# The last FFN's up-projection: seven products of quarters per block on halves of 256 tokens, in place of eight on 512 tokens

## The chip, the cores and the metric

The kernel runs on one core of one Trainium2 chip, as one launch. The metric is the device time in microseconds (us), and lower is better. Inputs and outputs are float32.

## What is computed

The reference is a two-layer backbone over 512 latent tokens and 256 context tokens, with a model width of 1024. Each layer holds an FFN, a mixing stage (DeltaNet heads and RWKV-7 heads) and a second FFN. In the second layer the context tokens leave the computation after the mixing stage, so the last of the four FFNs works on the 512 latent tokens alone:

```
def swiglu(h, w13, w2):
    gate, up = jnp.split(h @ w13, 2, axis=-1)
    return (jax.nn.silu(gate) * up) @ w2

h_lat = h_lat + 0.5 * m_lat[8] * swiglu(modulate(rms_norm(h_lat, norm_g[i, 2]), m_lat[6], m_lat[7]),
                                        ffn_w13[i, 1], ffn_w2[i, 1])
```

`w13` is 1024 x 5632 (gate and up, 2816 columns each) and `w2` is 2816 x 1024.

## The kernel before

**Layout.** Activations lie with model features on the 128 partitions and tokens along the free axis. A product of a 128x128 weight tile with up to 512 tokens is one matmul. To keep float32 accuracy every operand is split into a high part and a low part (both fp32r), and each product is made in three passes, high by high, high by low and low by high (`PASSES`). The high part is written by ScalarE (ACT, `act_piece`, L814) and the low part by VectorE (DVE, `dve_piece`, L821), which subtracts the high part from the raw weights in place.

**Blocks and parts.** The 2816 hidden features are 22 blocks of 128. The blocks are grouped into parts (`FF_PARTS`): part 0 has blocks 0 and 1, parts 1 to 5 have four blocks each. For each part TensorE (PE) first makes the blocks (the up-projection), then the part's share of the down-projection (`out`, L942), in two groups of four output tiles. DVE adds each output tile to `h` (`add`, L1201).

**Two ways of making a block.** The FFNs are numbered n = 0 to 3.
- The whole way (`whole_block`, L885 and L889): gate and up, eight weight tiles each, in three passes. In FFN 3, the one for which `lone(n)` is true, a product spans all 512 tokens: 2 x 8 x 3 = 48 matmuls of 512 columns for each block. In the other FFNs blocks 0 and 1 are made in this way, over two halves of 384 tokens.
- Seven pieces (`block`, L929): a block is a 2 x 2 matrix product (gate/up by lower/upper half of the model width) times (lower/upper width by left/right half of the tokens), and seven products of sums of quarters replace eight. Each piece is 4 tiles x 3 passes = 12 matmuls over half of the tokens, so a block is 84 matmuls. It is used for blocks 2 to 21 of FFNs 0, 1 and 2 (384 columns each).

**What the seven pieces need.** GpSimd (POOL, `pool_combine_weights`, L791 to L798) makes three weight combinations that PE uses and one step on the way, in four operations; ACT waits for the fourth before it splits the first piece. ACT and DVE split seven pieces for each block instead of four. At the head of an FFN DVE makes four sums of the activations (`sum_x`), and ACT and DVE split them (`x_high`, `x_low`); the last low part is made between the output additions of part 0. DVE needs nine combining operations over half of the tokens for each block (`combine`, L1116; `sum_2`, `sum_3`, ... `right_product`), where the whole way in FFN 3 needs one product over 512 tokens.

**Buffers and order.** Raw weights have two buffers, and a block's four loads of 256 KB (`block(f)` in `sp_ffn`, L733, issued by SyncE, SP) wait until PE has finished the block two before (`free`). The blocks in the first two places of a part are loaded partly under the down-projection of the part before (`early`, `late`); block 3 waits for the end of part 0's down-projection. Each engine has one fixed instruction order. For one block of seven pieces ACT's is

```
            def window(f):
                first_out(f)
                following(f, range(4))
                gate_left(f)
                following(f, (4, 5))
                gate_right(f)
                hidden_high(f, 9)
                following(f, (6,))
```

`following(f, ...)` splits the pieces of the next block. `first_out(f)` (L1005) copies the first product out of PSUM bank 0, and PE's fifth piece of the block, which writes that bank again, waits for it (`act_ready`). The sixth and seventh pieces wait for `sum_3` and `sum_4_and_up_right` on DVE. DVE's order is sums 2, 3, 4 and up-right, two splits, gate-left, two splits, up-left and left product, two splits, gate-right, right product, hidden-low, the last split.

Of the kernel before, what the change touches and what calls it, by code (L numbers as in the profile page):

```python
# [11 lines left out]
D_MODEL, SEQ, CTX, DEPTH, GRID_W = 1024, 512, 256, 2, 64  # L12
# [23 lines left out]
def build(nc, x, c, ctx, c_ctx, ada_w, ada_b, norm_g, ffn_w13, ffn_w2, w_in, dn_conv, dn_a_log, dn_dt_bias,  # L36
# [3 lines left out]
    with es:  # L40
# [578 lines left out]
        K_ORDER = tuple(k + KH * g for k in range(KH) for g in range(2))  # L619

        def lone(n):
            return n == 2 * DEPTH - 1

        def whole(n, f):

            return lone(n) or f < WHOLES
# [7 lines left out]
        def count_ffn():  # L634

            number, silus, sums, last_use = 0, 0, 0, {}
            for n in range(2 * DEPTH):
                sums += 0 if lone(n) else SUMMED_X
                load = 0
                for part, (f0, tiles) in enumerate(FF_PARTS):  # L640
                    for what in [*range(f0, f0 + tiles), (part, 0), (part, 1)]:
                        block = type(what) is int
                        piece_of[n, what], load_of[what] = number, load
                        load_first.append(number)
                        if block:
                            part_of[what] = part
                            silus_of[n, what], combined_of[n, what] = silus, sums
                            silus += 2 if lone(n) else 3 if whole(n, what) else 4
                            sums += 1 if lone(n) else 2 if whole(n, what) else 9
                        for j in range(pieces(n, what) if block else GROUP):  # L650
                            high = high_place(n, what, j)
                            high_free.append(last_use.get(high, -1) + 1)
                            last_use[high] = number
                            number += 1
                        load += 1
# [2770 lines left out]
```

## Time and profile before

| | |
|---|---|
| median of 3 runs | 3991.49 us (3987.45 to 3994.32) |
| profiled execution, span on the chip | 3987.0 us |
| PE busy | 3781.7 us (95%) |
| DVE busy | 2206.0 us (55%) |
| ACT busy | 1453.5 us (36%) |
| POOL busy | 760.9 us (19%) |
| mean granted TensorE clock | 0.991 |

The page gives the profiled execution's span alone, 4.5 us below the median of the runs. "Busy" is the share of the span in which an engine had an instruction in it. Matmuls are pipelined, so a matmul's own duration (389 ns for 512 columns) is longer than the distance from one start to the next. Times of rows are counted from the span's start. The granted clock is 1.00 at 2.4 GHz and 0.50 at 1.2 GHz. FFN 2 lies between about 2113 and 2667 us, FFN 3 between about 3595 and 3967 us.

### The profile page before, as it was taken

To read this page: it belongs to the slowest core of one execution; us is meant where nothing else is said; L and a number is where in the kernel's file an instruction comes from. 1 tells how busy PE (TensorE), PEld (TensorE's weight loads), DVE (VectorE), ACT (ScalarE), POOL (GpSimd) and SP (SyncE) were. 2 spreads that over 40 slices of the span, in tenths; PEclk is the share of its full clock that TensorE was granted. 3 is DMA by queue.
4 is the path that set the end of the run, shared out by engine and by line. 5 is a ranking of instruction groups with operands and counts; after the bars stand their busy time and mean duration, and the time that the engine had idled before them with its cause. 6 is when DMAs were issued, how large, how long until landed. Compare 5 with 4: busy or idle time off the path is not lost. (4 is left out here: it accounts for less than half of the span.)

```text
span 3987.0 us, 92656 instructions
## 1 busy us (share of the span) xinstructions
PE 3781.7 (95%) x40011; PEld 3300.6 (83%) x40011; DVE 2206.0 (55%) x3770; ACT 1453.5 (36%) x2512; POOL 760.9 (19%) x879
## 2 busy tenths in 40 slices
PE   7999999999988889999999999999999989889999
PEld 5899997877867768999998999987877857767887
DVE  4655556466465445755556555566465464454334
ACT  3333334344353333433234333343343253333223
POOL 1222210043024310222211222210242043300000
PEclk8999999999999999999999999999999999999999
DMA  6433332100200011332223333332100200023232
GB/s 209 129 108 113 107 96 87 37 18 2 77 11 4 5 72 43 118 98 89 85 67 116 106 109 113 106 106 59 28 2 18 71 2 5 33 84 89 81 114 66
DMA packets 409034, 287.17 MB, mean 72 GB/s; under 512 B 13438, under 2 KB 366180, under 8 KB 408164
## 3 DMA queue, kind: packets, MB, share of 16 engines
q1 hardware_dynamic: 408676, 281.86, 23.1%
q8 instruction: 290, 4.75, 0.5%
q14 instruction: 68, 0.56, 0.0%
HBM read 270.27 MB, written 11.53 MB: 71 GB/s over the span
## 5 line engine op out<-in xcount | busy, mean ns | idle before, releaser
L814 ACT ACTIVATE w_hi<-w_raw 128x512 fp32r<-128x512 f32 (+1 forms) x724 | 405.2, 612 | 649.6 <-POOL w_raw L798 349.2
L821 DVE TENSOR_TENSOR w_lo<-w_raw,w_hi 128x512 fp32r<-128x512 f32 (+1 forms) x724 | 484.9, 710 | 173.5 <-ACT w_hi L814 173.5
L929 PE MATMUL PS<-x_hi,w_hi 128*128 128x384 f32 x1680 | 562.7, 335 | 1.6 <-DVE hid_flat L1116 1.6
L929 PE MATMUL PS<-x_lo,w_hi 128*128 128x384 f32 x1680 | 561.3, 334 | 0.0
L929 PE MATMUL PS<-x_hi,w_lo 128*128 128x384 f32 x1680 | 561.2, 334 | 0.0
L1201 DVE SCALAR_TENSOR_TENSOR arena<-PS,mod,arena 128x256 f32<-128x256 f32 (+1 forms) x336 | 198.4, 632 | 332.5 <-PE PS L942 332.2
L1116 DVE TENSOR_TENSOR hid_flat<-hid_flat,PS 128x384 f32<-128x384 f32 (+1 forms) x454 | 246.2, 557 | 236.5 <-PE PS L929 153.3
L942 PE MATMUL PS<-hidden_hi,w_hi 128*128 128x256 f32 (+1 forms) x1232 | 342.3, 348 | 7.7 <-DVE hidden_lo L1168 5.7
L942 PE MATMUL PS<-hidden_hi,w_lo 128*128 128x256 f32 (+1 forms) x1232 | 337.5, 344 | 0.0
L942 PE MATMUL PS<-hidden_lo,w_hi 128*128 128x256 f32 (+1 forms) x1232 | 336.8, 343 | 0.0
L791 POOL TENSOR_TENSOR w_raw<-w_raw 128x512 f32<-128x512 f32 x60 | 85.0, 1417 | 1257.7 <-DMA w_raw<-in_ffn_w_dram 1172.9
L929 PEld LDWEIGHTS PS<-x_hi,w_hi 128*128 128x128 f32 x1680 | 315.4, 188 | 2.9 <-DVE hid_flat L1116 2.9
L929 PEld LDWEIGHTS PS<-x_lo,w_hi 128*128 128x128 f32 x1680 | 315.4, 188 | 0.2
L929 PEld LDWEIGHTS PS<-x_hi,w_lo 128*128 128x128 f32 x1680 | 315.4, 188 | 0.0
L942 PEld LDWEIGHTS PS<-hidden_hi,w_hi 128*128 128x128 f32 x1232 | 228.2, 188 | 64.5 <-issue 30.6
L942 PEld LDWEIGHTS PS<-hidden_lo,w_hi 128*128 128x128 f32 x1232 | 231.6, 188 | 29.1
L942 PEld LDWEIGHTS PS<-hidden_hi,w_lo 128*128 128x128 f32 x1232 | 231.4, 188 | 29.2
L2534 POOL TENSOR_TENSOR arena<-arena 128x256 f32<-128x256 f32 (+1 forms) x240 | 169.8, 728 | 262.5 <-ACT arena L2527 262.5
L1775 PEld LDWEIGHTS PS<-arena 128*128 128x128 f32 x1344 | 155.6, 192 | 16.9 <-DVE arena L2005 10.1
L1775 PE MATMUL PS<-arena 128*128 128x128 f32 x1344 | 161.4, 277 | 7.7 <-DVE arena L2005 7.7
L1302 PE MATMUL PS<-p_hi,pw_hi 128*128 128x256 f32 (+1 forms) x544 | 142.8, 344 | 4.6 <-DVE pw_lo L1295 2.9
L1302 PE MATMUL PS<-p_hi,pw_lo 128*128 128x256 f32 (+1 forms) x544 | 138.8, 337 | 0.0
(358 smaller groups left out, 7331.1 us busy)
## 6 DMA issues: line engine op xcount, KB each, us to landing
w_raw<-in_ffn_w_dram SPq DMA_DIRECT2D x512, 256.0 KB, 4.0
arena<-in_ada_w_dram SPq DMA_DIRECT2D x120, 512.0 KB, 5.9
arena<-in_w_in_dram SPq DMA_DIRECT2D x64, 512.0 KB, 3.9
arena<-in_ada_w_dram SPq DMA_DIRECT2D x6, 2048.0 KB, 14.0
arena<-in_w_out_dram SPq DMA_DIRECT2D x16, 512.0 KB, 4.3
h_save<-arena SPq DMA_DIRECT2D x16, 384.0 KB, 2.3
arena<-h_save SPq DMA_DIRECT2D x2, 3072.0 KB, 15.7
w_raw<-in_ffn_w_dram SPq DMA_DIRECT2D x32, 128.0 KB, 2.3
```

The costliest lines, as they stand in the source:

```text
L791: v.tensor_tensor(w[:, BOTH, :], w[:, DIFF, :], w[:, UP1, :], ALU.add).then_inc(weights_summed, 1)
L814: nc.scalar.activation(w_hi[:, high_place(n, what, j), 0:size], w_raw[:, load_of[what] % 2, place, 0:size], ACT.Copy).then_inc(w_high_read ...
L821: nc.vector.tensor_tensor(w_lo[:, b, place, 0:size], w_raw[:, b, place, 0:size], w_hi[:, high_place(n, what, j), 0:size].bitcast(F32), ALU ...
L929: mm = pe.matmul(PS[:, 4 * b + bank, 0:half], w[wo], x_split[xo][:, j, k, 0:half], start=(k == 0 and q == 0), stop=(k == KH - 1 and q == 2))
L942: mm = pe.matmul(PS[:, 2 * (k % 2) + s, 0:wd], w[wo], hid_split[xo][:, f, a0:a0 + wd], start=(f == 0 and q == 0), stop=(f == tiles - 1 and ...
L1116: v.tensor_tensor(out, x, y, op).then_inc(combined, 1)
L1201: ins = v.scalar_tensor_tensor(h[:, k, a0:a0 + w], PS[:, 2 * (k % 2) + s, 0:w], mod[:, c, at:at + 1], h[:, k, a0:a0 + w], ALU.mult, ALU.add)
L1302: mm = pe.matmul(PS[:, bank_ + s, 0:w], pw[wo][:, b, k * P:(k + 1) * P], x[xo][:, k, a:a + w], start=(k == 0 and q == 0), stop=(k == KT - ...
L1775: mm = pe.matmul(PS[:, b, u * P:(u + 1) * P], lhs[:, u, :], rhs[:, u, :], start=start and (stop or u == 0), stop=stop and (start or u == D ...
L2534: mult = lambda out_, a, b: gp.tensor_tensor(out_, a, b, ALU.mult)
```

## The change

`lone(n)` becomes false for every FFN. FFN 3 then takes the path of the other three: blocks 0 and 1 whole, but over two halves of 256 tokens; the sums of activations and their splits; blocks 2 to 21 in seven pieces over halves of 256 tokens, with POOL's four operations for each block, seven splits and nine combining operations on DVE. High parts of successive blocks then use the same seven places, where the whole way alternates between two sets of four (`high_place`). The down-projection is as before.

```
--- before.py
+++ after.py
@@ -619,7 +619,7 @@
         K_ORDER = tuple(k + KH * g for k in range(KH) for g in range(2))
 
         def lone(n):
-            return n == 2 * DEPTH - 1
+            return n < 0
 
         def whole(n, f):
 
```

## Rows read from the trace of the kernel before

**Rows 1.** Busy time by stretch: stretch, length, then each engine; granted clock near the end.

```profile
3600.00:3967.00 367.00, 361.96 (x1584) 296.49 (x1584) 156.35 (x243) 112.94 (x196) 0.00 (x0) 1.00 0.31 89
2178.00:2629.00 451.00, 449.74 (x2653) 419.97 (x2652) 256.99 (x435) 142.44 (x255) 102.97 (x76) 1.00 0.35 108
```

**Rows 2.** PE in order of time, four stretches: start us, us, instruction, count.

```profile
3703.09 0.39 PE L885 MATMUL PS<-x_hi,w_hi 128*128 128x512 f32 x1
...
3711.93 0.39 PE L885 MATMUL PS<-x_hi,w_hi 128*128 128x512 f32 x1
...
299.73 0.51 PE L942 MATMUL PS<-hidden_hi,w_hi 128*128 128x256 f32 x2
...
302.85 0.51 PE L942 MATMUL PS<-hidden_hi,w_hi 128*128 128x256 f32 x2
...
3597.81 2.17 PE L509 MATMUL PS<-ident 128*128 128x128 f32 x18
```

**Rows 3.** Groups of weight loads in FFN 3: count, busy us, mean ns, idle before.

```profile
L885 PEld LDWEIGHTS PS<-x_lo,w_hi 128*128 128x128 f32 x352 | 66.1, 188 | 13.5
```

**Rows 4.** Order of time in FFN 2, one block's weights, on SP, POOL, ACT and DVE.

```profile
2193.61 0.37 SPq L733 DMA_DIRECT2D w_raw<-in_ffn_w_dram  x1
...
2199.75 1.28 POOL L791 TENSOR_TENSOR w_raw<-w_raw 128x512 f32<-128x512 f32 x1 [10.25 <-DMA w_raw<-in_ffn_w_dram]
...
2205.05 2.20 ACT L814 ACTIVATE w_hi<-w_raw 128x512 fp32r<-128x512 f32 x4 [6.24 <-POOL w_raw L798]
...
2205.72 1.29 DVE L821 TENSOR_TENSOR w_lo<-w_raw,w_hi 128x512 fp32r<-128x512 f32 x2 [2.77 <-ACT w_hi L814]
...
2208.16 0.92 SPq L733 DMA_DIRECT2D w_raw<-in_ffn_w_dram  x2
...
2213.87 0.47 ACT L1005 ACTIVATE hid_flat<-PS 128x384 f32<-128x384 f32 x1
```

**Rows 5.** The same view, a little later: DVE and POOL at the same time.

```profile
2214.35 1.78 DVE L821 TENSOR_TENSOR w_lo<-w_raw,w_hi 128x512 fp32r<-128x512 f32 x1
...
2214.00 1.58 POOL L791 TENSOR_TENSOR w_raw<-w_raw 128x512 f32<-128x512 f32 x1 [8.98 <-DMA w_raw<-in_ffn_w_dram]
2215.66 1.62 POOL L793 TENSOR_TENSOR w_raw<-w_raw 128x512 f32<-128x512 f32 x1
```

**Rows 6.** Groups by form, FFN 3 and FFN 2: count, busy us, mean ns.

```profile
L821 DVE TENSOR_TENSOR w_lo<-w_raw,w_hi 128x512 fp32r<-128x512 f32 x116 | 73.1, 686 | 68.9 <-ACT w_hi L814 68.9
...
L821 DVE TENSOR_TENSOR w_lo<-w_raw,w_hi 128x256 fp32r<-128x256 f32 x4 | 1.5, 418 | 0.0
...
L1116 DVE TENSOR_TENSOR hid_flat<-hid_flat,PS 128x384 f32<-128x384 f32 x144 | 77.1, 550 | 56.3 <-PE PS L929 53.9 <-ACT hid_flat L1046 1.9
...
L814 ACT ACTIVATE w_hi<-w_raw 128x256 fp32r<-128x256 f32 x8 | 2.7, 406 | 4.0 <-DMA w_raw<-in_ffn_w_dram 4.0
```

**Rows 7.** Order of time in FFN 3, end of part 0 and start of part 1.

```profile
3627.16 0.37 SPq L733 DMA_DIRECT2D w_raw<-in_ffn_w_dram  x1
...
3630.09 1.15 ACT L814 ACTIVATE w_hi<-w_raw 128x512 fp32r<-128x512 f32 x2 [1.57 <-DMA w_raw<-in_ffn_w_dram]
...
3634.34 0.75 DVE L1201 SCALAR_TENSOR_TENSOR arena<-PS,mod,arena 128x512 f32<-128x512 f32 x1
...
3636.89 0.92 SPq L733 DMA_DIRECT2D w_raw<-in_ffn_w_dram  x2
...
3637.09 0.47 PE L885 MATMUL PS<-x_hi,w_hi 128*128 128x512 f32 x1 [0.23 <-DVE arena L1201]
...
3644.01 1.15 ACT L814 ACTIVATE w_hi<-w_raw 128x512 fp32r<-128x512 f32 x2 [11.72 <-DMA w_raw<-in_ffn_w_dram]
```

**Rows 8.** Idle times of PE elsewhere, and the stretches behind them with their granted clock.

```profile
3485.20 1.13 PE L2614 MATMUL PS<-arena 64*64 64x128 f32 x16 [2.34 <-issue]
...
38.47 0.72 PE L380 MATMUL PS<-pick,arena 128*128 128x2 f32 x5 [2.98 <-ACT arena L399]
...
3485.00:3488.00 3.00, 2.80 (x67) 2.79 (x68) 0.53 (x3) 0.00 (x0) 0.00 (x0) 0.50 1.07 447
38.00:42.00 4.00, 3.53 (x31) 2.00 (x31) 0.12 (x1) 1.49 (x3) 0.00 (x0) 1.00 1.05 387
```

## The prediction

> **What bounds the kernel now.** I read the table of busy time by stretch first. In the last FFN (FFN 3) PE is busy 361.96 of 367 us at a granted clock of 1.00, DVE 156.35 and ACT 112.94, while POOL does nothing [rows 1]. FFN 2 already runs the seven-piece path, and there PE is busy 449.74 of 451 us [rows 1]. So both ways are bound by PE at their present sizes, and the question is whether the seven-piece path still is when its products shrink from 384 to 256 columns. For that I read PE in order of time (what one product costs), and then followed one block's weights through FFN 2, on SP, POOL, ACT and DVE in order of time (what must fit beside one block).
>
> **The change, part by part.**
>
> *Products of blocks 2 to 21.* Products of 512 columns follow each other every 0.2267 us: 39 of them from 3703.09 to 3711.93 [rows 2]. No stretch has 256 columns alone, but the down-projection of FFN 0 alternates 256 and 512, and nine such pairs take 3.12 us, 0.3467 a pair, which leaves 0.1200 for the 256 [rows 2]. A lower bound is 0.111: eighteen products of 128 columns with their loads take 2.17 us, which I take as 17 distances and a last duration of 0.28 [rows 2]. An upper bound is 0.188, the duration of a weight load, if loads could not overlap each other [rows 3]. I take 0.120, since in the pairs the load behind each 256-column product was hidden. A block is then 84 x 0.120 = 10.08 us in place of 48 x 0.2267 = 10.88, and 20 blocks give back 16.0 us.
>
> A rule of the Trainium skill speaks against this: TensorE: Matmul & The Clock Gate, section "The mechanism", has weight loads overlap running matmuls only when they go to different row groups, and here each load fills the array. Read strictly, a block would pay 84 loads instead of 48 in the open, which is the last rival below; the pairs speak against it.
>
> *Blocks 0 and 1.* They become 96 products of 256 columns: 11.52 us each for 10.88, together +1.3 us.
>
> *From part 0 to part 1.* Now SP issues block 2's last quarter at 3627.16, ACT starts on it at 3630.09, 2.9 us later, and the first product of block 2 runs at 3637.09 [rows 7]. After the change the quarter is issued 1.3 us later (blocks 0 and 1). Then come 2.9 us of transfer, POOL's four operations, 5.3 us (2199.75 to 2205.05 [rows 4]), a high part, 0.6, and two low parts, 1.3 [rows 4]: 3638.6. Only then does DVE come to its sixth output addition, which now starts at 3634.34 [rows 7]. This is 4.25 us later, and PE waits for the seventh addition behind it before it starts block 2. I count +4.2 us, of which 1.3 is counted above, so +2.9. The sums of activations are hidden: seven DVE operations over 1024 elements (four sums, three low parts, with ACT's high parts beside them) at about 1.2 us, extended from 686 ns for 512 and 418 ns for 256 [rows 6], run while PE makes block 1. The fourth low part lies before the fifth addition, within the wait for POOL.
>
> *The weights' way.* A block's loads start when the block two before is finished; from there to the first low part ready in FFN 2 it takes 2205.72 + 0.69 - 2193.61 = 12.8 us [rows 4, 6]: 6.1 to POOL's start, 5.3 for POOL, 0.7 on ACT, 0.7 on DVE. With 0.2 until the first matmul it is 13.0. What covers it is one block. In FFN 2 that is 14.55 us (2193.61 to 2208.16 [rows 4]), so nothing shows. After the change it is 10.08: PE stands still for **2.9 us**. The pieces behind the first come faster than PE uses them.
>
> *A second wait in the same block.* ACT's copy `first_out` is queued behind all splits and the right-hand product of the block before. In FFN 2 it ends 2213.87 + 0.47 - 2205.05 = 9.3 us after POOL's end [rows 4]. At 256 columns four DVE combinations shrink by 0.13 each (550 to 418 ns [rows 6]) and the right product by 0.13; ACT's shorter copies and the hidden part take 0.4 more: 8.25 us. PE wants to begin the fifth piece at 1.4 + 0.2 + 4 x 1.44 = 7.3 us. So PE stands still again, **1.0 us** with its restart. DVE's sums for pieces six and seven end in time.
>
> *How often.* In parts 2 to 5 the blocks in the first two places are loaded under the down-projection, so the third block alone meets both waits. The fourth block's loads start while PE is held up and come in time, and after it comes a group with no work for POOL. In part 1 block 3 also starts its loads only at the end of the down-projection (3636.89, with 7.1 us until ACT can start [rows 7]), so blocks 3 and 5 meet them. That is 6 blocks x 3.9 = +23.4 us.
>
> *POOL beside DVE.* In five of the six the following block's POOL work runs beside the DVE chain of the second wait. In FFN 2 a low part of 0.69 us took 1.78 beside POOL, and POOL's operation 1.58 and 1.62 for 1.28 [rows 4 to 6]. Between 0 and 1.1 us for each of one or two operations; I take 0.8 for each block, +4 us (0 to 11). The Trainium skill (SBUF — State Buffer, "Who interferes with whom") says that a DVE instruction with two SBUF inputs and a GpSimd instruction that reads SBUF exclude each other, whoever is first keeping the port to its end. The 1.78 agrees.
>
> *The clock.* One idle time of 2.34 us was followed by a granted clock of 0.50 (1.2 GHz), another of 2.98 us by 1.00 [rows 8]. The six waits of 2.9 us lie there. Some 3.4 us at the lower level (0.213 us for a product, 256 columns at 1.2 GHz) would cost 1.5 us, part of it inside the second wait. I take +2 us, between 0 and 9.
>
> *Sum.* -16.0 + 1.3 + 2.9 + 23.4 + 4 + 2 = +17.6 us, on the profiled 3987.0 us: 4004.6. The median of the runs is 4.5 us above that span, so I forecast 3991.5 + 17.6 = **4009 us**.
>
> **The rivals.** A difference of 8 us (0.2%) is about the least that a measurement of this kernel can tell from none.
>
> *The waits are there but small.* In parts 1 to 5 the second wait hangs on an order of fifteen operations that I shrank from another size. Without it (-6), without interference and clock (-6), and with weights 0.3 us earlier (-2; the second load of FFN 2 took 5.84 us to POOL, 2208.16 to 2214.00 [rows 4, 5]), +3.6 remain: 3995 us, no change. For it: the order has slack in FFN 2. Against: the first wait alone is 2.9 x 6 = 17.4.
>
> *Faster: the weights' way hides.* If loads, POOL and both splits took at most the 10.1 us of a block, no block would wait, and -16.0 + 1.3 + 2.9 = -11.8 us: 3980 us. The point from which it decides is 2.9 us off 13.0. POOL alone takes 5.3 of these in every undisturbed row, and the loads 5.8 or more, so little speaks for it.
>
> *Weight loads bound the products.* If a load takes 0.188 us [rows 3] and cannot be overlapped by another, a block takes 84 x 0.188 = 15.8 us, longer than the 13.0 of the weights' way, all waits vanish, and 20 x 4.9 + 4 gives +102 us: 4094 us. Intermediate values also occur: each 0.01 us more for a product is +17 us, of which the waits of the six blocks swallow about half. Against it are the pairs and the 0.111 us of a 128-column product with its load.
>
> **How the numbers follow.** My forecast's case, slower by the weights' way, has 0.73. Waits too small to tell 0.12, faster 0.05, products held up by loads 0.10 (most of it small amounts above 0.120). Slower by over 0.2% is then 0.83, within 0.2% 0.12, faster 0.05. The range: its low end reaches to the case of small waits, +3.6 us, 3995. The high end has interference at 11, the clock at 9 and the rest as summed, -16.0 + 1.3 + 2.9 + 23.4 + 11 + 9 = +31.6, 4023, and some 6 us for products slightly above 0.120: 4029.
>
> **What would show it.** PE in FFN 3: L929 with 84 products of 256 columns for each block, 0.120 us apart. Before the third block of parts 2 to 5, and blocks 3 and 5, PE idles 2 to 4 us, released by DVE's low part (L821), and four pieces later about 1 us, released by ACT's L1005. ACT's idle before L814 is released by POOL L798. The distance from one part's first block to the next, now 66.0 us (3637.09 to 3703.09 [rows 2, 7]), becomes 67 to 69. Block 2 starts about 4 us later. The granted clock falls to 0.50 after some of these waits. The prediction is wrong if the distance between products is not 0.120, if POOL starts well before 6 us after the block's end, or if PE idles at other places, such as at the hidden parts at the start of a down-projection.

## The result, and the profile after

Four runs of the changed kernel have a median of 4020.1 us (4012.3 to 4032.2), against 3992.4 us for four of the kernel before on the same chip: a ratio of 1.0075, 95% interval 1.0059 to 1.0092. The forecast of 4009 us was 11 us low, within its range. The profiled execution took 4012.28 us, its span is 4010.6 us, 23.6 more than before.

All of it lies in FFN 3, from its first up-projection product to its last output product. This is the table of busy time by stretch of the changed kernel: length, PE, PEld, DVE, ACT, POOL, granted clock near the end.

```profile
3599.85:3990.35 390.50, 359.89 (x2400) 331.06 (x2400) 280.07 (x471) 157.16 (x300) 116.03 (x80) 0.98 0.29 84
3737.30:3750.60 13.30, 11.25 (x89) 10.85 (x90) 11.67 (x21) 7.18 (x16) 6.33 (x4) 1.00 0.21 60
```

The same stretch before, 3601.23 to 3966.82, is 365.6 us: FFN 3 is 24.9 us longer (and began 1.4 earlier). DVE's time went from 156 us [rows 1] to 280, POOL's from nothing to 116. The second row is part 2's third block, with its second waits (2.04 us) and 0.6 us of the block behind it: DVE is busy for 11.67 of 13.30 us. PE in order of time (start us, us):

```profile
3642.77 0.41 PE L929 MATMUL PS<-x_hi,w_hi 128*128 128x256 f32 x1
3642.98 0.41 PE L929 MATMUL PS<-x_lo,w_hi 128*128 128x256 f32 x1
...
3690.16 0.28 PE L929 MATMUL PS<-x_hi,w_lo 128*128 128x256 f32 x1
...
3691.96 0.28 PE L929 MATMUL PS<-x_hi,w_lo 128*128 128x256 f32 x1
```

From 3690.16 to 3691.96 are 15 distances, 0.120 us each, weight loads and all. At a granted clock of 0.50 (first two rows) the distance is 0.21. A block that doesn't wait takes 10.08 us; the first block of a part takes 10.3. What PE waited for in parts 1 to 5 (the waits: engine, releaser, us in total, times, longest):

```profile
PE PS L929 <- DVE w_lo L821: 15.1, 6, 3.1
PE PS L929 <- DVE hid_flat L1116: 4.9, 5, 1.0
PE PS L929 <- ACT hid_flat L1005: 3.6, 4, 1.3
```

The six waits for a low part are there, and four of the second kind. The middle row is one that the forecast had ruled out. Here is part 2's third block in order of time on SP, POOL, ACT, DVE and PE:

```profile
3724.99 12.09 SPq L733 DMA_DIRECT2D w_raw<-in_ffn_w_dram  x8
...
3730.60 1.29 POOL L791 TENSOR_TENSOR w_raw<-w_raw 128x512 f32<-128x512 f32 x1 [14.44 <-DMA w_raw<-in_ffn_w_dram]
...
3735.90 2.19 ACT L814 ACTIVATE w_hi<-w_raw 128x512 fp32r<-128x512 f32 x4 [7.04 <-POOL w_raw L798]
...
3736.56 1.29 DVE L821 TENSOR_TENSOR w_lo<-w_raw,w_hi 128x512 fp32r<-128x512 f32 x2 [5.05 <-ACT w_hi L814]
...
3737.31 0.39 PE L929 MATMUL PS<-x_hi,w_hi 128*128 128x256 f32 x1 [2.27 <-DVE w_lo L821]
...
3740.87 1.68 POOL L791 TENSOR_TENSOR w_raw<-w_raw 128x512 f32<-128x512 f32 x1 [5.00 <-DMA w_raw<-in_ffn_w_dram]
...
3743.53 0.99 DVE L1168 TENSOR_TENSOR hidden_lo<-hid_flat,hidden_hi 128x512 fp32r<-128x512 f32 x1 [0.70 <-ACT hidden_hi L1017]
...
3744.34 0.39 PE L929 MATMUL PS<-x_hi,w_hi 128*128 128x256 f32 x1 [1.01 <-ACT hid_flat L1005]
...
3747.07 0.38 PE L929 MATMUL PS<-x_hi,w_hi 128*128 128x256 f32 x1 [1.03 <-DVE hid_flat L1116]
```

The load is issued when the block two before ends, POOL starts 5.6 us later and takes 5.3, and the block begins 12.3 us after the issue, 2.27 us after PE ran dry. Then POOL's work for the fourth block begins at 3740.87 beside DVE, DVE's 0.69 us operations stretch (hidden-low took 0.99, and the split behind it 1.78), and PE stops twice more, for 1.01 and 1.03 us.

At the hand-over from part 0 to part 1, also in order of time:

```profile
3626.76 0.37 SPq L733 DMA_DIRECT2D w_raw<-in_ffn_w_dram  x1
...
3630.00 1.56 POOL L791 TENSOR_TENSOR w_raw<-w_raw 128x512 f32<-128x512 f32 x1 [151.55 <-DMA w_raw<-in_ffn_w_dram]
...
3632.43 1.63 DVE L1186 TENSOR_TENSOR x_lo<-w_raw,x_hi 128x1024 fp32r<-128x1024 f32 x1
...
3632.94 2.25 POOL L795 TENSOR_TENSOR w_raw<-w_raw 128x512 f32<-128x512 f32 x1
...
3636.59 3.75 ACT L814 ACTIVATE w_hi<-w_raw 128x512 fp32r<-128x512 f32 x7 [8.29 <-POOL w_raw L798]
...
3638.46 0.75 DVE L1201 SCALAR_TENSOR_TENSOR arena<-PS,mod,arena 128x512 f32<-128x512 f32 x1
...
3641.49 0.41 PE L929 MATMUL PS<-x_hi,w_hi 128*128 128x256 f32 x1
```

The order is the one that was forecast. But POOL took 6.6 us for its four operations, one of them 2.25 beside DVE's 1.63 (x_low of T3, the last of the four sums of activations to be split). PE stood still for 2.88 us before the last output tile (at 3639.35), the granted clock fell to 0.50 at 3640.01, and block 2 started 41.6 us after FFN 3 did, against 35.9 before [rows 7]: +5.8 in place of +4.2.

The distances of the parts' starts are 73.0, 68.0, 70.0, 68.3 us and 69.6 to the end (66.0 before, 65.9 in parts 2 to 4).

### The profile page after: what moved, and what is told of

It reads as the page before. It is cut to its first block and busy times, and to the rows that moved or that the text cites. A ratio compares the mean times of both kernels' runs of the same rounds, so it can differ in the third digit from the quotient of the medians.

```text
span 4010.6 us, 94943 instructions
## 1 busy us (share of the span) xinstructions
PE 3777.8 (94%) x40827; PEld 3334.1 (83%) x40827; DVE 2326.0 (58%) x4000; ACT 1499.2 (37%) x2618; POOL 875.6 (22%) x959
## 5 line engine op out<-in xcount | busy, mean ns | idle before, releaser
L929 PE MATMUL PS<-x_hi,w_hi 128*128 128x384 f32 (+1 forms) x2240 | 726.0, 324 | 24.3 <-DVE w_lo L821 15.1
L929 PE MATMUL PS<-x_lo,w_hi 128*128 128x384 f32 (+1 forms) x2240 | 722.9, 323 | 0.0
L929 PE MATMUL PS<-x_hi,w_lo 128*128 128x384 f32 (+1 forms) x2240 | 722.6, 323 | 0.0
L814 ACT ACTIVATE w_hi<-w_raw 128x512 fp32r<-128x512 f32 (+1 forms) x784 | 439.5, 612 | 642.4 <-POOL w_raw L798 442.3
L821 DVE TENSOR_TENSOR w_lo<-w_raw,w_hi 128x512 fp32r<-128x512 f32 (+1 forms) x784 | 547.9, 736 | 149.4 <-ACT w_hi L814 149.4
L791 POOL TENSOR_TENSOR w_raw<-w_raw 128x512 f32<-128x512 f32 x80 | 117.1, 1464 | 1605.0 <-DMA w_raw<-in_ffn_w_dram 1520.4
L929 PEld LDWEIGHTS PS<-x_hi,w_hi 128*128 128x128 f32 x2240 | 426.2, 190 | 29.0 <-DVE w_lo L821 16.3
L929 PEld LDWEIGHTS PS<-x_lo,w_hi 128*128 128x128 f32 x2240 | 426.1, 190 | 0.4
L929 PEld LDWEIGHTS PS<-x_hi,w_lo 128*128 128x128 f32 x2240 | 426.0, 190 | 0.0
L1116 DVE TENSOR_TENSOR hid_flat<-hid_flat,PS 128x384 f32<-128x384 f32 (+1 forms) x576 | 288.1, 516 | 175.6 <-PE PS L929 167.2
L942 PEld LDWEIGHTS PS<-hidden_hi,w_hi 128*128 128x128 f32 x1232 | 228.3, 188 | 68.8 <-issue 31.1
```

The source lines that it names most:

```text
L791: v.tensor_tensor(w[:, BOTH, :], w[:, DIFF, :], w[:, UP1, :], ALU.add).then_inc(weights_summed, 1)
L814: nc.scalar.activation(w_hi[:, high_place(n, what, j), 0:size], w_raw[:, load_of[what] % 2, place, 0:size], ACT.Copy).then_inc(w_high_read ...
L821: nc.vector.tensor_tensor(w_lo[:, b, place, 0:size], w_raw[:, b, place, 0:size], w_hi[:, high_place(n, what, j), 0:size].bitcast(F32), ALU ...
L929: mm = pe.matmul(PS[:, 4 * b + bank, 0:half], w[wo], x_split[xo][:, j, k, 0:half], start=(k == 0 and q == 0), stop=(k == KH - 1 and q == 2))
L942: mm = pe.matmul(PS[:, 2 * (k % 2) + s, 0:wd], w[wo], hid_split[xo][:, f, a0:a0 + wd], start=(f == 0 and q == 0), stop=(f == tiles - 1 and ...
L1116: v.tensor_tensor(out, x, y, op).then_inc(combined, 1)
```

## The experiments

All kernels differ from the changed one in FFN 3 alone. Code is shortened, with "..." for what is left out. Experiments 1, 2 and 8 leave out most of the weight combinations of eleven blocks. Times are medians beside the kernel before on the same chip. "FFN 3" is the length of its stretch in the profiled run, 365.6 before and 390.5 changed. The way (of the weights) is what lies between the issue of a block's loads and its first product. A first wait is one of PE before a block's first product, a second wait one before its fifth or sixth piece; contention is POOL and DVE slowing each other.

**1. Small combinations.** Neither the length of the way nor contention.

```
+ few = slice(0, 8) if n == 2 * DEPTH - 1 and under is None else slice(0, PIECE)
- v.tensor_tensor(w[:, BOTH, :], w[:, DIFF, :], w[:, UP1, :], ALU.add)
+ v.tensor_tensor(w[:, BOTH, few], w[:, DIFF, few], w[:, UP1, few], ALU.add)
...
+ if n == 2 * DEPTH - 1 and type(what) is int and what >= WHOLES and group_under(what) is None and place in (BOTH1, BOTH, LAST):
+     return spare[:, 0, :]
...
```

> The seven-product form stays everywhere. In the last FFN, for the eleven blocks whose quarters are not loaded under a down-projection (block 3 and the third and fourth of each later part), GpSimd's four combinations run over 8 of 512 columns, and the splits of three of the pieces read a tensor of zeros in their place; so most of those combinations of the weights are left out. Theory (the way of the weights, 13.0 us from a freed buffer to the next block's first product, is longer than a block of 10.1 us): the way falls to about 7.5 us (SyncE and DMA 6.1, a ScalarE and a VectorE split and their semaphores 1.4), so the first waits (sum 16.1 us in the trace of the changed kernel), the second waits (9.9) and the clock falls after them (some 7) all go, and VectorE's splits go back from 0.81 to 0.69 us. Only the late hand-over of the first part stays: about 4018 - 33 = 3980 to 3988 us, 0.992 of the changed kernel, faster than the kernel before. Rival (the smaller products themselves cost more than the columns say, by their weight loads or their issue): the distance of the parts stays near 70 us and the time at 4010 or more.

Measured: 3983.3 us, ratio 0.9982 (0.9972 to 0.9991). Stretch and waits of PE:

```profile
3608.23:3967.64 359.41, 351.86 (x2400) 325.63 (x2400) 269.68 (x471) 157.34 (x300) 63.80 (x80) 0.99 0.32 91
```

```profile
PE PS L953 <- DVE arena L1212: 4.5, 6, 2.9
PE PS L940 <- ACT hid_flat L1016: 0.5, 1, 0.5
```

All first waits are gone. The parts took 64.3, 63.7, 63.3, 62.9 and 63.1 us; four blocks of 10.08 and the 22.4 us that a down-projection had before make 62.7. So the products give back nearly what was forecast, and the rival that they are held up by loads fell. What the change costs above that, 31.1 us, hangs on POOL's combinations in eleven blocks. What remains is DVE's work. A stretch of 10.06 us at one third block, and behind it a block of the kernel before, in the table of busy time:

```profile
3734.84:3744.90 10.06, 9.58 (x80) 9.38 (x79) 8.80 (x20) 6.07 (x13) 1.09 (x4) 1.00 0.36 104
```

```profile
3725.00:3735.90 10.90, 10.90 (x50) 9.03 (x49) 3.88 (x6) 3.42 (x6) 0.00 (x0) 1.00 0.33 96
```

DVE has 8.80 us of work for a block of 10.1, with POOL nearly at rest; before it had 3.88 for 10.9.

**2. Small combinations, and four idle ones.** Contention put back in another place.

```
+ for q in range(4):     # behind the four small ones
...
+     v.tensor_tensor(spare[:, 3 + q % 2, :], spare[:, 1, :], spare[:, 2, :], ALU.add)
...
```

> As the kernel with the small combinations, and GpSimd besides adds two tensors of 512 columns four times in each of those blocks, with a result that nobody waits for: contention with VectorE and nothing else. Most combinations of the weights are left out as there. If the length of the way is the cause and contention only adds to it: within 3 us of the kernel with small combinations, with VectorE's splits of 512 columns back at a mean of 0.8 us. If contention between GpSimd and VectorE makes the waits by itself (VectorE's splits and sums late): 10 us or more above that kernel, towards 4010.

Measured: 4012.4 us, 1.0060 (1.0047 to 1.0073); FFN 3 387.1 us. DVE's splits in order of time, and PE's largest wait:

```profile
3737.23 1.77 DVE L839 TENSOR_TENSOR w_lo<-spare,w_hi 128x512 fp32r<-128x512 f32 x1
3738.93 0.41 DVE L1134 TENSOR_TENSOR hid_flat<-hid_flat,PS 128x256 f32<-128x256 f32 x1
3739.26 1.46 DVE L839 TENSOR_TENSOR w_lo<-w_raw,w_hi 128x512 fp32r<-128x512 f32 x1
3740.64 1.78 DVE L839 TENSOR_TENSOR w_lo<-spare,w_hi 128x512 fp32r<-128x512 f32 x1
```

```profile
PE PS L947 <- ACT hid_flat L1023: 17.0, 6, 4.0
```

My theory gave at most 3 us over experiment 1; in FFN 3 it was 28. Operations of POOL whose results nobody reads make PE wait nearly as long as the whole change did. The experiment isn't clean: the idle operations come at another place and fall on more of the splits than POOL's real ones (DVE is busy for 303 us of FFN 3 here, for 280 in the changed kernel).

**3. Products that hold PE.** For the price of the clock: 18 products of 128 columns ahead of the six blocks that wait.

```
+ for _ in range(held):
+     pe.matmul(PS[:, 4 * b, 3 * P:4 * P], ident[:, :], ident[:, :], start=True, stop=True)
```

> The changed kernel, and ahead of each of the six blocks that wait for their weights (3 and 5 of the first part, the third of each later part) TensorE does 18 products of 128 columns that nobody reads, into a bank that the block then overwrites. Each takes about 0.06 us, so 1.1 us of a wait of 2 to 3 us is filled and the idle time stays under that after which the clock fell. If the falls of the clock cost the some 7 us that the trace shows (five falls of about 3.4 us, half of it lost, some of it made up while the next weights come): 5 to 8 us less than the changed kernel, 4010 to 4014. If the time lost at the low clock would have gone into the next wait anyway (the weights set the pace, so that a slow product costs nothing): no change within 2 us.

Measured: 4024.2 us, 1.0091 (1.0078 to 1.0104); FFN 3 392.9. The 18 took 4.18 us, not 1.1: each is there as two matmul records, 0.11 us apart, where I had reckoned one of 0.06. Each group held its block up longer than the wait that it filled. Repeated with 5:

> The first holding kernel's 18 products took 4.2 us ahead of each block, longer than the waits (2 to 3 us) that they should fill, so that it mixed a later start with a higher clock. Here 5 of the same products, 1.16 us by that trace: shorter than every one of the waits. If the falls of the clock cost time of their own (some 9 us over the last FFN, by the changed kernel's trace): the falls at the first waits go and the last FFN takes 384 to 387 us in place of 390.5. If time lost at the low clock goes out of the following wait (the weights set the pace): falls gone, and the last FFN stays within 2 us of 390.5.

Measured: 4021.0 us, 1.0081 (1.0068 to 1.0095); FFN 3 396.9, which is neither the 384 to 387 nor within 2 us of 390.5, as the two theories had it. 2.3 us of it lie in a load of block 3 that took 8.2 us to land, and the clock fell twice in part 1, which took 77.7 us. The table of busy time of this kernel, parts 2 to 4:

```profile
3708.77:3776.94 68.17, 64.43 (x443) 59.60 (x442) 49.33 (x85) 26.82 (x52) 23.47 (x16) 1.00 0.33 93
3776.94:3846.45 69.51, 64.43 (x443) 59.60 (x442) 50.41 (x85) 26.81 (x52) 23.39 (x16) 1.00 0.33 92
3846.45:3915.97 69.52, 64.43 (x443) 59.59 (x442) 50.48 (x85) 26.81 (x52) 23.40 (x16) 1.00 0.32 91
```

There is no fall of the clock in these three, and they are not shorter than in the changed kernel (68.0 without a fall, 70.0 and 68.3 with one). Parts 2 to 4 of both holding kernels, with the changed kernel's part 2, are seven without a fall, 68.6 us on average; the two with one are 69.1. This doesn't give the price of a fall: the 18 products held their blocks up, and with 5 the second waits of parts 3 and 4 reached 2.2 us, against 1.0 at most in the same parts of the changed kernel. In the changed kernel itself the third block's period, from its first product to the next block's, was 12.7 us without a fall (part 2) and 13.8, 12.7 and 13.8 with one.

**4. Each split waits for its own combination.**

```
+ elif type(what) is int and not whole(n, what) and n == 2 * DEPTH - 1:
+     if j in (GATE0, GATE1, UP1):
+         act.wait_ge(landing(what), loaded(n, what))
+     else:
+         act.wait_ge(weights_summed, combos_done(n, what) - {BOTH: 3, DIFF: 2, BOTH1: 1, LAST: 0}[j])
...
```

> The changed kernel, but in the last FFN ScalarE and VectorE wait, for each piece, for the one combination that it needs (for the plain quarters on ScalarE: for the load alone) and no longer for the fourth. The first split can then start after GpSimd's first two operations, 2.7 us earlier. Theory (the way of the weights sets the six first waits): first waits of 2.7 us fall to 0 to 1 us, so that 8 to 15 us are won against the changed kernel and the clock falls in the last FFN go: 4003 to 4012. Rival (what limits is the last split and the sums of VectorE, behind GpSimd's last operation): the first waits turn into second waits in the same block, and less than 4 us are won.

Measured: 4007.3 us, 1.0048 (1.0035 to 1.0061); FFN 3 380.5. PE's waits:

```profile
PE PS L936 <- DVE w_lo L828: 10.1, 6, 2.0
PE PS L936 <- ACT hid_flat L1012: 6.1, 5, 1.5
PE PS L936 <- DVE hid_flat L1123: 5.0, 5, 1.0
```

10 us shorter, as the theory had it, but not as it had it: the first waits lost 5 us and the second ones gained 2.6. Block 2 starts 1.6 us sooner, and the clock fell once in place of five times; how the rest divides isn't shown. Each limit has another close behind it.

**5. Seven pieces only where the load is hidden.** Nine blocks of seven products; eleven, and blocks 0 and 1, of eight, over halves. The right half of x's first four k isn't kept in this layout, so the later eight-product blocks read the sum T3 in its place.

```
- return lone(n) or f < WHOLES
+ return lone(n) or f < WHOLES or n == 2 * DEPTH - 1 and (f == 3 or (f - 2) % 4 >= 2)
```

> The seven products only in the nine blocks of the last FFN whose quarters load under a down-projection; the other eleven there (2 of them too in the changed kernel: 0 and 1) by eight products over 256 tokens at a time, so without combinations of GpSimd between their load and their first product. Theory (the way of the weights with the four combinations in it makes the waits): none of the first and second waits of third and fourth blocks; the nine blocks win 0.8 us each against the kernel before (7.2 in all), the whole blocks lose 0.7 each over halves (some 7.7 for eleven), the late hand-over of the first part stays (+4): the last FFN takes 366 to 371 us against 365.6 before and 390.5, the time 3990 to 3997. Rival (the seven-product blocks under the down-projections lose as much as the others): waits of several us stay in those, the last FFN takes over 375.

Measured: 3995.1 us, 1.0015 (1.0006 to 1.0023); FFN 3 372.9. No wait in any block; all that remains in parts 1 to 5 is at output additions:

```profile
PE PS L944 <- DVE arena L1216: 1.6, 5, 0.3
```

That is 2 us over the upper end stated: block 2 came 6.3 us later than before (I had counted 5.4), the first seven-product block of a part takes 10.3 us and not 10.08, and the expectation counts blocks 0 and 1 among the eleven, where they come on top. Parts 2 to 5 took 65.8 us, 0.1 less than before. The blocks that load under a down-projection keep their gain.

**6. Early landing.** The quarters land in tensors of their own; POOL works from there. The way is short, contention stays.

```
+ if staged(n, f):
+     raw = stage[f % 2]
+     pool.wait_ge(stage_landed[f % 2], STAGE_BASE + 64 * stage_turn(f))
+     pool.wait_ge(piece_used, load_first[LOADS * n + load_of[f] - 1])
+     v.tensor_tensor(w[:, BOTH, :], raw[:, 1, :], raw[:, 3, :], ALU.add)
```

> The changed kernel, but the quarters of block 3 and of the third and fourth block of each later part land in tensors of their own, a block or more ahead; GpSimd reads them there when the buffer two blocks back comes free. So SyncE and the DMA (some 6 us) leave the way of the weights, and GpSimd's four operations over 512 columns, beside VectorE, stay. If the length of the way is the cause: the way is some 7 us against a block of 10.1, first and second waits go but for up to 1 us at the last splits, and the last FFN takes 364 to 371 us, the time 3985 to 3993. If contention between GpSimd and VectorE is the cause, as the kernel with four idle GpSimd operations per block suggests (387 us): it takes 378 or more.

Measured: 4004.3 us, 1.0041 (1.0025 to 1.0056). The stretch, then PE's waits in parts 1 to 5:

```profile
3599.10:3982.36 383.26, 359.52 (x2400) 331.94 (x2400) 295.59 (x471) 157.28 (x300) 120.58 (x80) 0.97 0.30 86
```

```profile
PE PS L970 <- ACT hid_flat L1046: 10.0, 5, 2.3
PE PS L970 <- DVE hid_flat L1157: 3.9, 5, 0.8
PE PS L970 <- DVE w_lo L862: 2.4, 1, 2.4
```

The theory that the length of the way is the cause gave 364 to 371, and it fell. Five of the six first waits are gone, and second waits have taken their place. One third block in order of time shows how:

```profile
3733.12 1.48 POOL L819 TENSOR_TENSOR w_raw<-stage 128x512 f32<-128x512 f32 x1
3733.37 3.48 DVE L862 TENSOR_TENSOR w_lo<-stage,w_hi 128x512 fp32r<-128x512 f32 x2
...
3738.30 0.63 ACT L1058 ACTIVATE hidden_hi<-hid_flat 128x512 fp32r<-128x512 f32 x1 [0.68 <-DVE hid_flat L1157]
...
3739.36 0.36 ACT L1046 ACTIVATE hid_flat<-PS 128x256 f32<-128x256 f32 x1
```

Two splits take 3.48 us in place of 1.37. DVE's sums and product come behind them, ACT's hidden part waits for these, and `first_out` of the next block is queued behind it; its end releases PE, 2.29 us late. DVE has little room to make that up (a stretch of 12.60 us at this block, with PE's idle time in it; DVE is busy for 11.35):

```profile
3730.70:3743.30 12.60, 10.31 (x75) 10.11 (x74) 11.35 (x19) 5.40 (x12) 6.04 (x4) 0.88 0.00 0
```

In parts 2 to 5 the clock also fell after this wait, and the third block's period was 14.1 us. In the next kernel the wait is the same 2.29 us in parts 2 to 5, and the period is 14.1 in the three with a fall and 12.6 in part 4 without one, so there a fall did cost 1.5.

One thing makes this kernel more than the changed one with a shorter way: POOL's combinations now start when the buffer comes free and fall on DVE's splits. DVE is busy for 296 us of FFN 3, against 280 in the changed kernel and 270 in experiment 1.

**7. Early landing and own combinations together.** The edits of 4 and 6.

> The kernel with the early landing, and ScalarE and VectorE wait for the combination that each piece needs and no longer for the fourth. By the length of the way nothing is left for it to win in third and fourth blocks but up to 1 us at each, and 1.5 us at the hand-over of the first part, as in the kernel that had this alone: the last FFN takes 362 to 369 us, the time 3983 to 3991. By contention the gain is the one that this step alone had (10 us less than with the early landing).

Measured: 4003.3 us, 1.0037 (1.0024 to 1.0050); FFN 3 378.6. By the median that is no more than 6, within what is measured, and far from the 362 to 369 that the length of the way gave. The trace shows 1.9 us less at the hand-over and one fall less. DVE is as busy as in experiment 6 (301 us).

**8. Length alone.** Small combinations, with two fills of zeros ahead of them.

```
+ for q in range(2):
+     if f > 3 or q:
+         pool.wait_ge(ada_used, at + q)
+     nc.gpsimd.memset(spare[:, 1:6, :], 0.0).then_inc(ada_used, 1)
...
```

> The length of the way alone: the kernel with the small combinations (most combinations of weights left out), and between the landing of the quarters and the small combinations GpSimd fills 2560 columns with zeros twice. One such fill took 2.23 us in that kernel's trace, so that GpSimd's part of the way is 5.3 us again, as in the changed kernel, but nothing of it reads two tensors beside VectorE. With the kernel with small combinations (last FFN 359.4 us: neither), the early landing (383.2: short way, combinations beside VectorE) and the changed kernel (390.5: both) it makes a square. If the length of the way makes first waits of its own: six of 2 to 3 us, the last FFN takes 372 to 380 us. If contention (VectorE's own work per block over 10.1 us beside GpSimd) is all of it: 359 to 363. If the fills slow VectorE too (its splits at 0.8 us or more), this doesn't tell them apart.

Measured: 4009.2 us, 1.0046 (1.0031 to 1.0060). The stretch, PE's wait, and the fills (groups of POOL):

```profile
3602.97:3986.18 383.21, 357.71 (x2400) 330.57 (x2400) 270.49 (x471) 157.40 (x300) 112.53 (x102) 0.98 0.30 86
```

```profile
PE PS L946 <- DVE w_lo L838: 17.5, 6, 3.7
```

```profile
L804 POOL MEMSET spare<- 128x2560 f32 x22 | 49.2, 2236 | 102.3 <-DMA w_raw<-in_ffn_w_dram 101.7
```

Six first waits, 2.9 us on average, and one second wait of 0.8. FFN 3 is 3 us over the upper end stated (380); with the waits came five falls of the clock, and PE was busy 5.9 us longer than in experiment 1. DVE's busy time is that of experiment 1, 270 us. The fills don't slow DVE: twelve splits that ran for more than half of their time beside a fill took 0.68 us each, as alone. So this is the length alone, with the falls that its waits bring. It also says something of the second waits: with the length alone one of them is left, so it takes POOL's sums beside DVE to make the 8.5 us of the changed kernel. The Trainium skill (SBUF — State Buffer, "Who interferes with whom") has a DVE instruction with two SBUF inputs contend with a GpSimd instruction that reads SBUF and not with one that only writes it. The traces agree on both sides: 0.68 us beside a fill, and 1.48 on average for the 47 splits of experiment 6 that ran beside POOL's sums of two tensors.

The four kernels make a square (FFN 3 in us):

```
                           combinations not beside DVE    beside DVE
way short                  359.4 (experiment 1)           383.3 (experiment 6)
way 13 us long             383.2 (experiment 8)           390.5 (changed kernel)
```

Each alone costs 24 us, both together 31. They don't add up. One reading is that while PE waits for the one, the other catches up. The square is not a clean one: the contention of experiment 6 is larger (26 us more of DVE's busy time than in experiment 1) than that of the changed kernel (10 us more), so 24 us is the price of contention as it falls in experiment 6.

**9. Seven pieces in eight blocks, 512 columns elsewhere.** The version that the experiments point to. x's first four k lie whole, so that the eight-product blocks again stream 512 columns.

```
+ return lone(n) or f < WHOLES or n == 2 * DEPTH - 1 and (f <= 3 or (f - 2) % 4 >= 2)
...
+ if n == 2 * DEPTH - 1:
+     x = x_wide[xo][:, k, :] if k < KH else x_places(xo, n, k, half)
+     to = PS[:, 4 * b + 2 * g, 0:2 * half]
+     if k >= KH:
+         to = to.rearrange("p (s t) -> p s t", s=2)
+     mm = pe.matmul(to, w[wo], x, start=(first_k and q == 0), stop=(last_k and q == 2))
```

> The seven products only where the kernel with halves showed no wait (first and second block of the four later parts, whose quarters load under a down-projection; not block 2), and all other blocks of the last FFN by eight products over 512 tokens as in the kernel before; the first four k of x lie whole in a tensor of their own for that. By the traces: a part of four blocks takes 65.8 us with its whole blocks over halves, of which 1.3 us go with 512 columns, against 66.0 in the kernel before: 64.5; blocks 0 and 1 and the hand-over of the first part as in the kernel before. The last FFN takes 359 to 361 us against 365.6, the time 0.9980 to 0.9990 of the kernel before. Rival: VectorE's sums of a seven-product block run into the whole block behind it, or the hand-over gets a new wait: the last FFN at 364 or more, no gain that can be measured.

Measured: 3985.5 us, ratio 0.9982 (0.9970 to 0.9994): 0.2% faster than the kernel before. FFN 3 is 4.5 us shorter than before and 29 us shorter than in the changed kernel. Part 1 (eight products in all blocks), part 2, and FFN 3:

```profile
3639.75:3705.74 65.99, 65.67 (x288) 54.05 (x289) 29.37 (x45) 20.01 (x39) 10.60 (x7) 1.00 0.40 112
3705.74:3770.29 64.55, 64.21 (x362) 56.17 (x360) 39.27 (x65) 22.81 (x44) 11.96 (x8) 1.00 0.35 98
3602.97:3964.09 361.12, 357.09 (x1872) 305.11 (x1872) 216.64 (x351) 133.11 (x252) 47.96 (x32) 1.00 0.32 91
```

A part with two seven-piece blocks takes 64.5 us against 66.0, four times 1.4 in all, and the hand-over gives 0.9 back.

## Why the prediction was right, and where it was not

The direction and its main place were right; point by point, with FFN 3's own sums:

- **Products, -16.0**: nearly. They are 0.120 us apart and an undisturbed block takes 10.08, but the first block of each part takes 10.3, which leaves about 15. Experiment 1's parts 2 to 5 come within 0.2 to 1.0 us of the 62.7 that 10.08 gives. The lower bound of 0.111 was misread: its eighteen records are nine products, since a 128-column product of the f32 identity shows as two records (experiment 3). The 0.120 didn't rest on it. The rule of the Trainium skill that the forecast named (TensorE: Matmul & The Clock Gate, "The mechanism", loads overlap only for other row groups) has the trace against it: full loads whose records last 0.19 us are hidden at 0.120 us a product. The same section also lets a load go ahead when it targets the background weight buffer, which no run here tells apart.
- **Blocks 0 and 1, +1.3**: 1.4.
- **From part 0 to part 1, +2.9**: 4.4 (5.8 with blocks 0 and 1). POOL's operations took 6.6 us and not 5.3, beside x_low of T3 on DVE. I had laid POOL's rows of an undisturbed stretch beside a DVE that was busy. The low clock behind PE's wait of 2.88 us adds some 0.6.
- **First waits, 6 x 2.9 = 17.4**: 16.1 counted in the same way (15.1 idle), at exactly the six blocks; experiment 8, which has the length alone, shows 17.5. In part 1 the blocks start 13.0 us apart three times, which is the way of 13.0.
- **Second waits, 6 x 1.0 = 6.0**: 9.9, counted from product to product with PE's restarts (8.5 us idle). Four waits hang on `first_out` (3.6 us idle), but "DVE's sums for pieces six and seven end in time" fell: five waits hang on them (4.9 us). The cause given was off too: the term came from the order of operations alone, and experiment 8, which has that order and the length but no sums of POOL beside DVE, has one such wait of 0.8 us.
- **POOL beside DVE, +4 (0 to 11)**: the size was within its bounds: the changed kernel's FFN 3 is 7.3 us over experiment 8's, which has the length alone. The kind was wrong. I priced some operations that stretch, on a path, on top of the waits. The runs show that contention can hold PE up by itself: experiment 6 has it with a short way, and costs 24 us. My reading is a second limit of the block's period: in the stretches shown DVE has 8.8 us of work in 10.06, and 11.35 in 12.60 with POOL's four combinations beside it, which is more than a block of 10.08. No run tells a DVE that is full from one that is late at one place in its order.
- **The clock, +2 (0 to 9)**: five falls in FFN 3, and PE was busy 8.0 us longer than in experiment 1. What the falls cost net in the changed kernel stays open, between nothing and 8 us: its third blocks with a fall took 1.1 us more than the one without in two cases and nothing more in the third.
- **The sum**: +24.9 in FFN 3 (+23.6 on the span) against +17.6. Parts 1 to 5 came out 19.1 us longer, so with the 16.0 of the products everything else in them took 35.1 us, where the forecast's terms had 29.4; the hand-over adds 1.6 with blocks 0 and 1. That the forecast is this close is in part luck: the second waits and the contention were wrong in kind and about right in size. The medians lie 27.7 us apart, since the profiled run was the shortest of the changed kernel's four.
- **The faster rival** was put wrongly, although it had little chance. It would decide, I wrote, when the way is 2.9 us shorter. Experiment 6 shortened it by more, and the kernel took 4004 us: a short way alone doesn't hide the waits while POOL's sums run beside DVE's splits.

The distances of the parts, forecast at 67 to 69, were 68.0 to 70.0, and 73.0 in part 1, where three blocks in a row pay the way.

## What to carry to other kernels

When a change makes the bounding engine's block shorter, lay against the new block not only the chain that leads to it but the full work of every other engine, with contention counted in. FFN 2's rows gave an estimate of DVE's before any run: seven splits and hidden-low at 0.69 us and nine combinations at 0.42 are 9.3 us against 10.1, and one split took 1.78 beside POOL. To find which of two such limits is the cause, build the kernel without either as well as each alone; taking away one of them won 7 us here where both were worth 31. And a scheme need not be taken everywhere: in the blocks whose load lies under other work it won 0.6 to 0.8 us each, while of those before which PE waits it made distances of 12.5 to 13.8 us in place of 10.9.

## What the runs showed of the hardware

- Splits of DVE took 0.68 us each beside a POOL that filled 2560 columns with zeros (2.24 us a fill, experiment 8), as with POOL at rest; beside POOL's sums of two tensors single ones took 1.78.
- Products of 256 columns, each with its own weight load of 128 columns, follow each other every 0.120 us, though the loads' records last 0.19 us. Each product of 128 columns of an f32 identity that experiment 3 issued shows as two matmul records, 0.11 us apart.
- In the changed kernel's FFN 3 idle times of PE of 2.5 to 3.1 us came with a fall of the granted clock to 0.50 (at their end or within 1.1 us of it) five times, those of 1.9 and 2.3 us did not. In experiment 2, 2.6 and 3.0 us were followed by no fall, and in experiment 6 an idle time of 2.3 us was followed by one four times.
- A load of 1 MB that took 6.0 us to land in most blocks took 8.2 once (experiment 3 with 5 products).
